# First two weight chunks taken row by row of x, squares dealt over four units, modulation sums turned in 32x32 blocks

## What is computed

```
h = rmsnorm(x, norm_g);  proj = h @ w_in          # 2048 x 14336
v, bg, cg, za, u, zb, ga, gb = split(proj)
ya = (bg * conv3(cg * v) * silu(za)) @ w_out_a
yb = gelu(s5_scan(u));  yb = yb * sigmoid(yb @ w_glu + b_glu)
yb = (yb * silu(zb)) @ w_out_b
x1 = rmsnorm(x + (sigmoid(ga) * ya + sigmoid(gb) * yb) @ w_o, final_g)

shift, scale, gate = split(silu(c) @ w_ada + b_ada, 3)   # 2048 x 6144, one row
h2 = rms_norm(x1, norm_g_2) * (1 + scale) + shift;  z = h2 @ w_in_2
y = [spatial gating(z) | forgetting attention(z)]
out = rms_norm(x1 + gate * (y @ w_out_2), final_g_2)
```

## Time and profile before

| | us |
|---|---|
| median of 3 runs | 2540.23 (2539.63 to 2540.47) |
| the profiled execution, its own time | 2540.18 |
| its span in the trace | 2538.9 |
| PE busy | 2509.5 (99%) |
| DVE busy | 1652.3 (65%) |
| ACT busy | 842.2 (33%) |
| POOL busy | 401.9 (16%) |
| DMA queue 1, share of 16 engines | 41.6% |
| mean granted TensorE clock | 0.992 |

### The profile page before, as it was taken

The page is one execution under the profiler, slowest core; times in us unless marked ns, Lnnn a source line. Parts: engine busy times, 40 slices in busy tenths (PEclk is TensorE's granted clock), DMA queues, the critical chain, the costliest instruction groups (busy, mean ns, idle before and its releaser), DMA issues.

```text
span 2538.9 us, 30018 instructions
## 1 busy us (share of the span) xinstructions
PE 2509.5 (99%) x11928; PEld 2174.9 (86%) x11928; DVE 1652.3 (65%) x2187; ACT 842.2 (33%) x1139; POOL 401.9 (16%) x295
## 2 busy tenths in 40 slices
PE   9999999999999999999999999989999999999997
PEld 7888888888888888888888888878888888888886
DVE  6789888999988776545545775557555553244534
ACT  5222222222222222233322333332556564333321
POOL 0045343444444340000000000020000000000001
PEclk9999999999999999999999999989999999999998
DMA  5233333333333433767556675523322222322333
GB/s 193 97 120 120 113 122 113 122 113 121 115 109 131 134 125 123 244 213 253 197 198 212 215 236 202 196 102 133 100 83 84 84 84 86 118 97 96 118 125 116
DMA packets 119867, 353.07 MB, mean 139 GB/s; under 512 B 15408, under 2 KB 22832, under 8 KB 119728
## 3 DMA queue, kind: packets, MB, share of 16 engines
q1 hardware_dynamic: 119728, 351.16, 41.6%
HBM read 321.68 MB, written 23.07 MB: 136 GB/s over the span
## 4 chain that ended last, share of the span: by engine, by line
PE 97%; DVE 1%; DMA 1%; ACT 0%; issue 0%; SPq 0%; DVEq 0%
PE bank L526 29%; PE bank L527 29%; PE bank L528 29%; PE bank L693 2%; PE bank L694 2%; PE bank L695 2%; PE bank L736 1%; PE bank L726 1%; DMA W<-in_w 1%; PE bank L591 1%; PE bank L579 1%; DVE SO L1436 0%; PE bank L717 0%; PE bank L719 0%; PE bank L516 0%; DVE X L1838 0%
## 5 line engine op out<-in xcount | busy, mean ns | idle before, releaser
L1155 DVE TENSOR_TENSOR WL<-W,WH 128x1024 fp32r<-128x1024 f32 (+1 forms) x456 | 608.1, 1337 | 464.6 <-ACT WH L831 463.7
L831 ACT ACTIVATE WH<-W 128x1024 fp32r<-128x1024 f32 (+1 forms) x456 | 478.1, 1051 | 913.4 <-PE bank L528 680.9
L526 PE MATMUL bank<-hH,WH 128*128 128x512 f32 x1792 | 682.2, 381 | 2.2 <-DVE hL L1425 2.2
L527 PE MATMUL bank<-hL,WH 128*128 128x512 f32 x1792 | 680.2, 380 | 0.0
L528 PE MATMUL bank<-hH,WL 128*128 128x512 f32 x1792 | 680.2, 380 | 0.0
L526 PEld LDWEIGHTS bank<-hH,WH 128*128 128x128 f32 x1792 | 339.2, 189 | 58.7 <-issue 6.3
L528 PEld LDWEIGHTS bank<-hH,WL 128*128 128x128 f32 x1792 | 339.3, 189 | 48.6
L527 PEld LDWEIGHTS bank<-hL,WH 128*128 128x128 f32 x1792 | 339.5, 189 | 47.8
L526 PE MATMUL bank<-h2H,WH 128*128 128x512 f32 x640 | 245.5, 384 | 0.1
L527 PE MATMUL bank<-h2L,WH 128*128 128x512 f32 x640 | 242.6, 379 | 0.0
L528 PE MATMUL bank<-h2H,WL 128*128 128x512 f32 x640 | 242.6, 379 | 0.0
(11 more groups left out here) (260 smaller groups left out, 3589.5 us busy)
## 6 DMA issues: line engine op xcount, KB each, us to landing
W<-in_w SPq DMA_DIRECT2D x335, 512.0 KB, 3.7
W<-in_ada SPq DMA_DIRECT2D x96, 512.0 KB, 4.3
W<-in_wa SPq DMA_DIRECT2D x32, 512.0 KB, 4.1
W<-in_wo SPq DMA_DIRECT2D x32, 512.0 KB, 3.9
W<-in_wvv SPq DMA_DIRECT2D x32, 512.0 KB, 3.7
W<-in_wb SPq DMA_DIRECT2D x16, 512.0 KB, 3.8
URAW<-U SPq DMA_DIRECT2D x96, 64.0 KB, 3.0
scr_am<-SO SPq DMA_DIRECT2D x16, 256.0 KB, 2.0
```

Of the source, the lines that this page charges most:

```text
L526: e.matmul(o, wh, xh, start=first, stop=False)
L527: e.matmul(o, wh, xl, start=False, stop=False)
L831: e.activation(WH[:, n % NB, c], W[:, i % NW, c], ACT.Copy).then_inc(sem["hi"], 1)
L1155: e.tensor_tensor(WL[:, s, c], W[:, plan.item_of[n] % NW, c], WH[:, s, c].bitcast(F32), ALU.subtract).then_inc(sem["lo_v"], 1)
```

## The change

Four things, in `program` and the engines' programs:

- The left halves of units 0 and 1 are both loaded first (`w_first`, now two semaphores), the right halves later. PE takes rows 0 to 7 of x one at a time and multiplies each by unit 0 into projection 0's bank and by unit 1 into projection 1's, then units 2 and 3 as before. ACT and DVE prepare the right halves ahead of rows 4 and 5, unit 2 ahead of row 9.
- The 16 squares and their sums have a `unit()` after row 2, 7, 12 and 15. `token_sums` moves from ahead of unit 5 to ahead of unit 7, `spread` from unit 6 to unit 8, `keep_u` of the first projections by one projection; so u takes six banks, and all later projections are one bank further round.
- DVE turns ACC in 32x32 blocks three units ahead of each reduction, and adds up each block's 32 columns to AR (128 x 32). Its next part may then overwrite ACC.
- PE's eight matmuls with ACC as weights become four with SEL (128 x 32: four identities under one another) as weights and eight columns of AR moving, each into its own 32 partitions of bank 3.

```diff
-U_BANKS = (0, 1, 2, 4, 0, 1, 2, 0)
+U_BANKS = (0, 1, 2, 4, 5, 6, 0, 1)
+SQUARES = (2, 7, 12, 15)
...
+    SEL = at("SEL", 196, [128, 32])
+    AR = at("AR", 196.125, [128, 32])
+    AT = [T[:, 2:4, :].rearrange("p a b -> p (a b)"), U[:, 0:2, :].rearrange("p a b -> p (a b)")]
...
-        e.dma_start(W[:, 0, 0:512], plan.items[0][:, 0:512]).then_inc(sem["w_first"], 16)
         for i, (k, k_end) in enumerate(X_PARTS):
-            if i in (1, 4, 6):
+            if i < 2:
+                e.dma_start(W[:, i, 0:512], plan.items[i][:, 0:512]).then_inc(w_first[i], 16)
+            if i in (3, 4, 6):
                 fetch()
...
-                e.wait_ge(*nth("ada_v", cb))
+                e.wait_ge(*nth("ada_r", cb))
...
-                for q in range(8):
-                    mm = e.matmul(bank[3][:, q:q + 1], ACC[:, 128 * q:128 * q + 128], ONE[:, 0:1],
-                                  start=True, stop=True)
+                parts = AR[:, :].rearrange("p (q g) -> p g q", g=4)
+                for g in range(4):
+                    mm = e.matmul(bank[3][32 * g:32 * g + 32, 0:8], SEL[:, :], parts[:, g, :], start=True, stop=True,
+                                  skip_group_check=True)
...
-        for kc in range(2):
+        at_unit[0] = 2
+        for k in range(8):
+            h_ready(k)
             for p in range(2):
-                n = unit()
-                products(n, u_p[p], kc, 0, 15, xh, xl, h_ready if p == 0 else None)
+                if k == 0:
+                    e.wait_ge(*nth("lo_first", p))
+                if k == 4:
+                    e.wait_ge(*lo_done[p])
+                c = slice(128 * k, 128 * k + 128)
+                mm = triple(bank[bank_of[u_p[p]]][:, :], WH[:, p, c], WL[:, p, c], pairs(xh(k)), pairs(xl(k)),
+                            k == 0, False)
+                if k == 7:
+                    mm.then_inc(sem["used"], 1)
+        for p in range(2):
+            products(unit(), u_p[p], 1, 0, 15, xh, xl, h_ready if p == 0 else None)
...
-            if n == plan.units(u_p[2])[1]:
+            if n == plan.units(u_p[3])[1]:
...
-            if n == plan.units(u_p[3])[0]:
+            if n == plan.units(u_p[4])[0]:
...
-                    e.wait_ge(*nth("mod", i // 16 - 1))
+                    e.wait_ge(*nth("ada_t", i // 16 - 1))
...
+        def ada_sums(cb):
+            turned = AT[cb // 4]
+            if cb == 0:
+                e.tensor_reduce(SEL[:, :], IDT[:, :].rearrange("p (r a) -> p a r", r=4), AX,
+                                ALU.add).then_inc(sem["sel"], 1)
...
+            e.wait_ge(*nth("ada_v", cb))
+            e.transpose(turned, ACC[:, :]).then_inc(sem["ada_t"], 1)
+            e.wait_ge(*nth("ada_t", cb))
+            if cb > 0:
+                e.wait_ge(*nth("ada_pe", cb - 1))
+            e.tensor_reduce(AR[:, :], turned.rearrange("p (c b) -> p c b", b=32), AX,
+                            ALU.add).then_inc(sem["ada_r"], 1)
...
+            if n + 3 in plan.reduce_at:
+                ada_sums(plan.reduce_at[n + 3])
```

More of the change, by code:

```diff
@@ L145, in program @@
     sem = {n: nc.alloc_semaphore("s_" + n) for n in SIGNALS}
+    w_first = [nc.alloc_semaphore(f"w_first{i}") for i in range(2)]
     w_in = [nc.alloc_semaphore(f"w_in{i}") for i in range(NW)]
@@ L302, in program @@
         read[p] = [(sem["ug_a"], i + 1)]
-    bank_of, bank_free, n, before = {}, {}, U_BANKS[-1] + 1, [[], [], [], [], []]
+    bank_of, bank_free, n, before = {}, {}, U_BANKS[-1] + 1, [[] for _ in range(7)]
     for p, (stage, _) in enumerate(plan.projections):
@@ L881, in act_program @@
         root_table()
-        e.wait_ge(*nth("w_first", 0))
-        e.activation(WH[:, 0, 0:512], W[:, 0, 0:512], ACT.Copy).then_inc(sem["hi_first"], 1)
-        e.wait_ge(sem["par"], 16)
         for k in range(16):
-            if k in (1, 5, 11):
-                hi({1: 0, 5: 1, 11: 2}[k])
+            if k < 2:
+                e.wait_ge(w_first[k], 16)
+                e.activation(WH[:, k, 0:512], W[:, k, 0:512], ACT.Copy).then_inc(sem["hi_first"], 1)
+            if k == 0:
+                e.wait_ge(sem["par"], 16)
+            if k in (4, 5, 9):
+                hi({4: 0, 5: 1, 9: 2}[k])
             i = [k in range(*part) for part in X_PARTS].index(True)
@@ L897, in act_program @@
             e.activation(T[:, k % 4, :], XS[:, k, :], ACT.Square).then_inc(sem["xsq"], 1)
-            if k % 8 == 7:
-                unit()
-        for m, p in enumerate(u_p[2:]):
+            if k in SQUARES:
+                ssm_until(unit())
+        for m in range(3, 8):
             ssm_until(unit())
-            if m == 1:
+            if m == 4:
                 e.wait_ge(*nth("spread", 0))
@@ L1415, in ssm_until @@
                 done[0] += 1
[L1417 to L1420, removed]
         for k in range(16):
[L1422 to L1423 removed]
+            if k < 2:
+                e.wait_ge(*nth("hi_first", k))
+                e.tensor_tensor(WL[:, k, 0:512], W[:, k, 0:512], WH[:, k, 0:512].bitcast(F32),
+                                ALU.subtract).then_inc(sem["lo_first"], 1)
+            if k == 0:
+                e.wait_ge(sem["par"], 16)
+            if k in (4, 5, 9):
+                lo({4: 0, 5: 1, 9: 2}[k])
             e.wait_ge(*nth("xh", k))
@@ L1443, in keep_u @@
                             ALU.mult).then_inc(sem["u_rd"], 1)
-        for m in range(2, 8):
+        for m in range(3, 8):
+            ssm_until(unit())
+            if m == 4:
+                e.wait_ge(*nth("rsa", 0))
+                for i in range(4):
+                    keep_u(i)
             ssm_until(unit())
             if m == 3:
[L1448 to L1452, removed]
                 inv_rms(0, 3, 0, 0)
```

28 lines of the change are left out of this document (12 added, 16 removed).

## The result

| | before | changed |
|---|---|---|
| median | 2540.35 (2539.63 to 2540.58, 4 runs) | 2526.86 (2526.14 to 2528.15, 4 runs) |
| ratio, 95% interval | | 0.9948 [0.9931, 0.9965] |
| the profiled execution, its own time | 2540.18 | 2528.15 |
| its span | 2538.9 | 2526.9 |
| PE busy | 2509.5 | 2497.0 |

The time is in us, and a ratio is to the kernel before. The kernel became faster by 13.5 us between medians, by 12.0 between the profiled executions; 10.75 were forecast. A second set of runs gave 2526.91 (2526.79 to 2527.56, 5 runs) against 2539.16 (2538.24 to 2540.38, 9 runs), ratio 0.9952 [0.9938, 0.9965].

What follows compares the result with a forecast made beforehand. PE was taken as the bound, 97% of the chain of waits. Gains of 3.1 + 0.9 + 7.4 + 0.65 less 1.3 made 10.75 us, from 2540.18 to 2529.4 us; range 2527.0 to 2535.0.

Steps and rivals of the forecast that it cites:

- The start, 3.1 us: Up to unit 4: six matmuls per row instead of three start unit 4 at 31.0 instead of 34.1, gaining 3.1 us.
- The rival of a clock that falls as before: At the start: the granted clock drops as before, 1.8 us less gained, 2531.2 us; chance 0.27.
- The lower level costs about 3.4 us: Old start, 11.4 to 17.5 us: the granted clock of 0.50 was said to cost PE about 3.4 us.
- The token sums, 0.9 us: Token sums after unit 4: PE's wait for a WL behind eight additions of squares goes, gaining 0.9 us.
- The reductions, 7.4 us: Six reductions on PE: each falls from 1.78 to 0.55 us, saving 7.4 us, bounds 3.8 and 8.9.
- I take 0.55 us per reduction: PE's new group of eight small instructions: 0.55 us assumed per reduction, between bounds of 0.3 and 1.15.
- the lower bound of 0.3: PE's cost per reduction if only the switches count: 0.3 us.
- The rival of "one after another": Reductions: the small matmuls run serially at 1.15 us per reduction, total 2533.0 us; chance 0.13.
- DVE's work, +1.3 us at the fourth reduction: DVE's 2.44 us of new work delays a BL in stage wg; PE waits 1.3 us there, other reductions covered.
- the rival of a slow one: DVE's transposition takes four passes, 4.9 us; the fourth reduction costs 3.7 us more, total 2533.1 us; chance 0.07.
- Banks, 0.65: Second seq pair: projections one bank further round shrink PE's wait from 0.94 to 0.3 us, gaining 0.65 us.

Runs made afterwards that it cites:

- e8_old_start_filled: The changed kernel with the old order of the first four units, plus 5, 3 and 4 filling matmuls ahead of rows 1, 2 and 5: 2528.08 us, one run.
- e5_squares_two: The changed kernel with the 16 squares in two portions of eight as before, token sums at their new place: 2531.32 us in one run.
- e2: The changed kernel with PE summing ACC as before and DVE's transposition and summing left out: 2534.36 us, ratio to before 0.9979.
- e3: The changed kernel with DVE's transposition and sums two units ahead of each reduction instead of three: 2526.26 us, ratio to before 0.9947.
- e10: The changed kernel with unit 3's load ahead of five parameter loads and DVE's new work one unit later: 2524.99 us, ratio to before 0.9945.
- e11: e10 with 22 matmuls on the identity around the token sums and spreading ahead of the first seq pair: 2523.8 us, ratio to before 0.9939.
- e9_after_again: The changed kernel run once more, unaltered, in turn with two further kernels; its profiled execution took 2526.79 us.

## Why the prediction came out so

- **The start, 3.1 us: right in size** (3.12), with its path (WL of unit 3 at 25.7, unit 4 at 31.0). The nearness to the hundredth is luck: with the same start, unit 4 begins at 30.7 to 31.6 in six profiles. The rival of a clock that falls as before is refuted: the granted clock is 1.00 from 7.6 us to beyond 1660 us in all ten profiles with the new order. What stood behind it was only partly right. "The lower level costs about 3.4 us", as the prediction put it for the old start, was mis-sized as a share of the gain: with the clock at 1.00 and the old order the gain is 1.5 us (e8_old_start_filled), since for the other 1.9 us PE would have waited for rows anyway: in e8_old_start_filled it still sits idle for 0.79 and 0.97 us on hL of x, besides its filling matmuls. The order of the rows gives the other 1.7.
- **The token sums, 0.9 us: right** (0.97), and too small a description of that part: with its portions alone undone, unit 6 starts 3.8 us later (e5_squares_two).
- **The reductions, 7.4 us: the mis-sized term.** "I take 0.55 us per reduction" measured 0.35, near the lower bound of 0.3, so the six gave 8.6. The readout that I leaned on carries streams of 512 columns, and its remainder isn't a price for groups of eight. Doubling the group (0.06 us for eight more instructions) shows that little but the switch is left. The rival of "one after another", at 1.15 each, is refuted by the changed kernel's 0.35 and by the same run.
- **DVE's work, +1.3 us at the fourth reduction and nothing at the others: right** in its cause, by luck in its size (1.20 in the first profile; PE's idle time there lies between 0.31 and 1.96 us in the eight profiles with DVE's work at this place, and unit 264 is 0.6 to 2.2 us longer; so this term is a range and not a number). Where it is gone, in e2, e3, e10 and e11, unit 264 takes the same 5.18 us as before the change. The transposition is an ordinary pass of 1.24 us, and the rival of a slow one is refuted; the rule that it moves one element per cycle per lane (Trainium skill, Vector Engine (DVE) Microarchitecture Reference, The reshape front-end and per-opcode configuration) agrees with that.
- **Banks, 0.65: right** (0.72).
- **Not in the sum**: the stretch from 306 to 320, where the low clock begins at a slightly different place of PE's work in each execution. Units 312 and 320 move by up to 1.4 us with it. The profiled execution of the changed kernel was the slowest of its four (2528.15, 1.3 over the median) and had this stretch at its worst; that is the difference between 12.0 and 13.5 us, as far as the profiles show it.
- **Why the median fell below the range.** The profile of e9_after_again (2526.79) stands for the median, and its span is 13.4 us below the one before. Against the forecast's 10.75 that is 2.6 more: 1.1 from the reductions, 0.8 from the stretch from 306 to 320 (99.5 against 100.4 us), 0.5 from a wait in unit 264 of 0.8 instead of 1.3, and 0.2 from the small terms. The low end of the range, 2527.0, had room for the first and the third, and none for the second. Whether the 0.8 is due to the change is open, with a single profile of the kernel before.

What stays open: why the low stretch begins where it does; no run here changes its start while leaving PE's work alone.

## What to carry to other kernels

Where a start is bound by arrival, put as much work as possible over each arriving row before trying to repair the clock; here the clock then stayed up by itself, and what it gave back must be measured with the order held fixed. A reduction over partitions that only needs a few columns is cheap on PE if another engine first folds the data; its price here was the switch, paid per group and hardly per instruction. New work on a covered engine should go behind the last result that PE waits for, not ahead of it: here one unit later was worth 0.8 to 1.2 us.

## What the runs showed that I had not expected

- PE's first matmul started anywhere from 6.5 to 8.0 us in different executions with the same start (6.53, 6.48, 7.10, 7.95, 8.00), and unit 2 started at 18.5 to 19.0 in all of them: the time is caught up while rows arrive. One more, e2_old_reduction, started at 7.01 and reached unit 2 at 19.39.
- The two profiled executions of the changed kernel differ mainly beside the stretch in which the clock is at 0.50, around the token sums of the middle: steps of 0.7 to 1.4 us at single units there, 0.4 in unit 264 and at the end, and nothing elsewhere.
- 22 matmuls of 128 columns that compute nothing kept the clock at 1.00 through a stretch that is otherwise at 0.50 for 10 to 17 us, and gained 1.2 us by medians, 0.9 by the unit starts.
